# Four weight sums in buffers of their own, and a ring of three places for the rounded weights of the feed-forwards

## The reference

```python
def swiglu(h, w_in, w_out):
    g, u = jnp.split(h @ w_in, 2, axis=-1)
    return (jax.nn.silu(g) * u) @ w_out

def decoder_layer(x, c, params, ...):
    mod = jax.nn.silu(c) @ mod_w + mod_b          # 9 x 1024 columns of modulation
    ...
    h = modulate(rmsnorm(x, norm_pre[0]), sh0, sc0)
    x = x + 0.5 * gt0 * rmsnorm(swiglu(h, ffn1_in, ffn1_out), norm_post[0])
    ...                                           # token mixing, then swiglu again
```

## Time and profile before

| | us |
|---|---|
| three runs: median (range) | 3004.87 (3000.71 to 3007.12) |
| profiled execution, its own time | 2993.15 |
| its span | 2991.4 |
| the four feed-forwards within it | 427.6, 428.3, 422.9, 402.9 |

### The profile page before, as it was taken

One profiled execution on the slowest core, in us unless ns is written; L12 is line 12 of the kernel. 1 busy time (PEld: TensorE's weight loads), 2 busy tenths in 40 slices (PEclk: granted clock), 3 DMA queues, 4 the chain that ended last, 5 costly groups with the idle time before them and its releaser, 6 DMA issues.

```text
span 2991.4 us, 52877 instructions
## 1 busy us (share of the span) xinstructions
PE 2748.0 (92%) x21498; PEld 2534.2 (85%) x21498; DVE 2072.3 (69%) x3716; ACT 1205.2 (40%) x2025; POOL 802.0 (27%) x591
## 2 busy tenths in 40 slices
PE   6999989999999998999898899999999999898988
PEld 4898988898776798899888898989987768898987
DVE  2656577887877576655785656888877956857574
ACT  4433234545363253332343332445543523433232
POOL 4141322133053031414131414130420520424230
PEclk8999999999999989999999999999999999899999
DMA  7555453222224343544533444441212333332432
GB/s 255 156 169 172 142 165 101 86 59 62 64 66 134 117 129 113 171 140 136 148 99 114 155 129 125 135 134 50 64 51 66 97 115 118 99 99 59 111 79 92
DMA packets 451724, 342.19 MB, mean 114 GB/s; under 512 B 24793, under 2 KB 403025, under 8 KB 449690
## 3 DMA queue, kind: packets, MB, share of 16 engines
q1 hardware_dynamic: 446074, 313.64, 35.3%
q0 software_dynamic: 5408, 25.17, 2.5%
HBM read 319.00 MB, written 19.76 MB: 113 GB/s over the span
## 4 chain that ended last, share of the span: by engine, by line
PE 51%; DVE 26%; issue 9%; DMA 7%; ACT 5%; SPq 0%; POOL 0%; ACTq 0%; DVEq 0%; POOLq 0%
PE PS L1482 51%; DMA stage<-in_ffn_in 5%; DVE lo_apart L2176 3%; ACT w_hi L992 3%; DVE hidf L2399 2%; DVE lo_over L2176 1%; DVE score L2801 1%; DVE best L2800 1%; DVE xT L2275 1%; DVE tmpn L2273 1%; DVE sq L2284 1%; DVE h_full L2322 1%; DVE W L2731 1%; DVE hid L2336 1%; DVE sil L2404 1%
## 5 line engine op out<-in xcount | busy, mean ns | idle before, releaser
L1482 PE MATMUL PS<-h_hi,w_hi 128*128 128x260 f32 x2720 | 702.4, 301 | 49.8 <-DVE hidf L2396 15.2
L1482 PE MATMUL PS<-h_lo,w_hi 128*128 128x260 f32 x2720 | 672.3, 290 | 0.0
L2176 DVE TENSOR_TENSOR lo_apart<-stage,w_hi 128x1024 fp32r<-128x1024 f32 (+1 forms) x312 | 482.6, 1550 | 272.1 <-ACT w_hi L992 270.6
L992 ACT ACTIVATE w_hi<-stage 128x1024 fp32r<-128x1024 f32 (+2 forms) x450 | 442.0, 990 | 482.5 <-PE PS L1482 233.7
L1482 PEld LDWEIGHTS PS<-h_hi,w_hi 128*128 128x128 f32 x2720 | 485.6, 197 | 99.4 <-issue 46.7
L1482 PEld LDWEIGHTS PS<-h_lo,w_hi 128*128 128x128 f32 x2720 | 485.7, 197 | 0.0
L1482 PE MATMUL PS<-hid,w_hi 128*128 128x260 f32 x2816 | 453.3, 283 | 8.0 <-DVE hid L2336 8.0
L1482 PE MATMUL PS<-h_hi,lo_apart 128*128 128x260 f32 x1536 | 431.6, 295 | 0.0
L1482 PEld LDWEIGHTS PS<-hid,w_hi 128*128 128x128 f32 x2816 | 385.6, 188 | 11.7 <-DVE hid L2336 9.3
L3207 POOL TENSOR_TENSOR sum<-stage 128x1024 f32<-128x1024 f32 x40 | 95.8, 2394 | 795.4 <-DMA stage<-in_ffn_in 412.0
L1482 PEld LDWEIGHTS PS<-h_hi,lo_apart 128*128 128x128 f32 x1536 | 300.8, 202 | 0.0
(11 more groups left out here) (470 smaller groups left out, 5234.1 us busy)
## 6 DMA issues: line engine op xcount, KB each, us to landing
stage<-in_ffn_in SPq DMA_DIRECT2D x176, 512.0 KB, 5.2
mod_stage<-in_mod_w SPq DMA_DIRECT2D x128, 512.0 KB, 6.1
stage<-in_w_in SPq DMA_DIRECT2D x72, 512.0 KB, 3.8
stage<-in_ffn_out SPq DMA_DIRECT2D x64, 512.0 KB, 6.0
x_hold<-xT SPq DMA_DIRECT2D x6, 2080.0 KB, 6.8
stage<-in_ffn_out SPq DMA_DIRECT2D x32, 384.0 KB, 3.4
mod_open<-in_mod_w SPq DMA_DIRECT2D x16, 512.0 KB, 9.7
stage<-in_w_out SPq DMA_DIRECT2D x16, 512.0 KB, 3.6
```

The lines of the kernel that those rows point to most:

```text
L992: nc.scalar.activation(by_tile(highs(ch), ch), weights(ch), ACT.Copy).then_inc(hi_done, 1)
L1482: return nc.tensor.matmul(out, lhsT, rhs, start=start, stop=stop)
L2176: nc.vector.tensor_tensor(by_tile(lows(ch), ch), weights(ch), by_tile(highs(ch), ch).bitcast(FP32), ALU.subtract).then_inc(lo_done, 1)
```

## The change

Every feed-forward chunk gets its place in the rings from the planner. Direct trips still use places 0 to 3; win trips and output tiles use places 0, 1, 2 in turn (number modulo 3). Chunk n is then rounded when PE has used chunk n-3. ACT and DVE run two chunks ahead and not three. The fourth place of `w_hi` holds the new `sum3`, the fourth place of `lo_apart` the new `sum4`. So S3 and S4 no longer overwrite staged weights: gate slots are free after the remainder of A12, up slots after that of A22, both only when all four sums are formed. SP still loads 1, 3, 0, 2. POOL waits for all four tiles before its first sum; S4 waits no longer for the remainder of A12; after a direct trip or output tiles, S3 waits until PE has used every earlier chunk. The turns move behind A12 (`turns[1]`) and behind S4 (`turns[5]`).

```diff
+    def in_ring(ch, slot):
+
+        ch.ring_slot, ch.after = slot, rounded_last[slot]
+        rounded_last[slot] = ch.base + 1
+        ring.append(ch)
...
                     for kind in OPERANDS:
-                        ring.append(Chunk(len(ring), BLK, kind, trip=t))
+                        in_ring(Chunk(len(ring), BLK, kind, trip=t), len(ring) % 3)
                     for q in range(4):
-                        freed[q] = ('lo', t.ring + (5 if q % 2 else 6))
+                        freed[q], summed[q] = ('lo', t.ring + (5 if q % 2 else 2)), SUMS * win_count
                     if pending is not None:
-                        t.turns[0], pending = pending, None
+                        t.turns[1], pending = pending, None
                     for j in ((), (6,), (3, 6))[per_trip[trip_no]]:
                         if pending is not None:
-                            t.turns[4], pending = pending, None
+                            t.turns[5], pending = pending, None
...
             for _ in range(KD):
-                staged(n * P)
+                staged(n * P, slot=len(ring) % 3)
...
+    sum3 = over("sum3", [P, 2, 512], ring0 + 7 * BLK * 4)
+    sum4 = over("sum4", [P, 2, 512], big0 + 3 * BLK * 4)
...
+                    if load.sums is not None:
+                        sp.wait_ge(sums_formed, load.sums)
...
-                    if ch.base >= 4:
-                        act.wait_ge(chunk_used, ch.base - 3)
+                    if ch.after is not None:
+                        act.wait_ge(chunk_used, ch.after)
...
                 def win(which, t, before):
                     end = ffn_end(which)
                     for j in range(7):
-                        advance(t.ring + j + 3, end)
+                        advance(t.ring + j + 2, end)
...
-                            for slot in (1, 3):
+                            for slot in range(4):
                                 pool.wait_ge(stage_full[slot], t.loads[slot].arrival)
                             pool.tensor_tensor(sum1[:], A21, A22, ALU.add).then_inc(sums_formed, 1)
-                            for slot in (0, 2):
-                                pool.wait_ge(stage_full[slot], t.loads[slot].arrival)
+                            if t.prev != 'win':
+                                pool.wait_ge(chunk_used, t.ring)
+                            pool.tensor_tensor(sum3[:], A11, A21, ALU.subtract).then_inc(sums_formed, 1)
                             pool.wait_ge(sums_formed, n + 1)
-                            pool.tensor_tensor(A21, A11, A21, ALU.subtract).then_inc(sums_formed, 1)
                             pool.tensor_tensor(sum2[:], sum1[:], A11, ALU.subtract).then_inc(sums_formed, 1)
                             pool.wait_ge(sums_formed, n + 3)
-                            pool.wait_ge(lo_done, t.ring + 2)
-                            pool.tensor_tensor(A12, A12, sum2[:], ALU.subtract).then_inc(sums_formed, 1)
+                            pool.tensor_tensor(sum4[:], A12, sum2[:], ALU.subtract).then_inc(sums_formed, 1)
```

More of the change, by code:

```diff
@@ L132, in staged @@
         ch.load = load
-        freed[last] = ('used' if in_place else 'lo', ch.base + 1)
-        ring.append(ch)
+        freed[last], summed[last] = ('used' if in_place else 'lo', ch.base + 1), None
+        in_ring(ch, len(ring) % 4 if slot is None else slot)
         return ch
@@ L150, in ffn_plan @@
                 if t.kind == 'direct':
-                    for _ in range(4):
-                        staged(BLK)
+                    for q in range(4):
+                        staged(BLK, slot=q)
                     a, d = a + 2, d + 2
@@ L156, in ffn_plan @@
                     win_count += 1
-                    t.loads = {q: loaded(q) for q in (1, 3, 0, 2)}
+                    t.loads = {q: loaded(q) for q in range(4)}
                     t.y, t.x, t.v = banks
@@ L1106, in direct @@
                                              ACT.Silu).then_inc(ev_a, 1)
-                        advance(t.ring + 4 + m, end)
+                        if m == 0:
+                            advance(t.ring + 4, end)
                     operand_hi(which, 0)
@@ L1111, in direct @@
                     operand_hi(which, 1)
-                    advance(t.ring + 6, end)
                     hid_high(slice(1, 2), slice(0, TOK), hidf[:, 1:2, :], t.ed + 2)
@@ L1141, in ffn_out @@
                     for m in range(KD):
-                        advance(part.ring + m + 3, ffn_end(which))
+                        advance(part.ring + m + 2, ffn_end(which))
                         if m == 0:
```

24 lines of the change are left out of this document (12 added, 12 removed).

## The result

The changed kernel takes 3031.38 us (median of 8 runs, 3024.24 to 3036.12), the kernel before 3005.32 (8 runs, 2999.91 to 3018.06). The ratio is 1.0082, with an interval of 1.0064 to 1.0099: slower by 26 us, where 3003 was forecast and 3025 was the upper end of the range.

What follows compares the result with a forecast made beforehand. The prediction took a ring through SP, ACT and DVE, with DVE late and not PE, as the bound; -18 + 8 - 4 + 9 - 4 + 6.7 = -2.3 us on 3004.87 gave 3003, range 2975 to 3025.

Steps and rivals of the forecast that it cites:

- the first term: 18 trips within a part, with modulation: 27.4 us for 28.4, together -18 us.
- a ring of 26.8 to 27.3: Within a trip, from one landing of gate weights through DVE and POOL's work and the loads to the next, in us.
- The wait of S3's sum for PE's last output tile: Behind output tiles: the remainders' chain runs late, 2 us each four times behind parts of six, 0.3 behind parts of eight.
- S4 waits for nothing: In a trip's ring: named as one of two edits that gain, beside A22's evictions ahead of A11's remainder; no separate size.
- PE's idle time stands somewhere anyway; the turn is where it shows.: In the feed-forwards: PE would hardly get back the 82.8 us of idle time ahead of the turns.
- the gain that follows it in size: Behind each direct trip, the stretch to the second S2: 26.5 us for 31.7 on average, -5.1 each.
- the output borders: Eight stretches across output tiles: +9 us, bounds 0 to +40.
- the stop between the second and third feed-forward: ACT and DVE stop where a direct trip's first chunk shares place 0 with the last output tile: +6.7 us.
- The slower one: In each trip: the wait for A12 is longer and the clock falls behind it; +28 us, 3031; chance 0.14.
- own case: Whole kernel: 3003 us, own range 2990 to 3016, with PE idle 3.2 us ahead of A12 each trip; chance 0.52.
- The turn is as late as before: At the turns: S3 stands ahead of `modrow`, the 18 trips with modulation stay at 28.4 us; 3020; chance 0.12.
- The faster one: In the trips: the ring is shorter than worked out, towards PE's busy time; 38 us off, 2965; chance 0.22.

Runs made afterwards that it cites:

- f1: The change with the first sum waiting for the up tiles only and S4's sum waiting for A12's remainder again; 2980.1 us.
- d1: The change's ring of three places and turns, but sums as before, S3 and S4 overwriting staged weights; 2961.1 us.
- e6: The change with the small matmuls of a modulation group moved behind the next trip's A11; 3026.6 us.
- f3: The change with only S4's sum waiting for A12's remainder again; 3035.4 us.
- e7: The change with POOL's first sum waiting for the two up tiles only, the second for the gate tiles; 3011.6 us.
- b1: The kernel before with only the turns moved, behind A12 and behind S4; 2958.7 us.
- e4: The change with the third feed-forward's direct trip using places 3, 0, 1, 2 instead of 0, 1, 2, 3; 3031.0 us.
- e5: The change with direct trips' first three chunks in the turn of three, the fourth in place 3, and A12 rounded within the direct trip; 3018.5 us.
- e2: The change with POOL's sum S2 waiting for the remainder of A12; 3065.1 us.

## Why the prediction was wrong

The forecast for the profiled execution was 2990.9, and it took 3031.0. Of these 40 us, 22 are in the first term and 18 in the others and the rest; some 12 need not be the change's, as said above.

**The step that failed in the sum: a trip with modulation was put at 27.4 us, by a ring of 26.8 to 27.3; it took 28.6, 18 times.** The ring was too short in three places, read from the trace after:

- *The wait of S3's sum for PE's last output tile.* The prediction priced it across the output tiles only (that term came out right). It also moves the next loads. It shows best without modulation. In the 2 stretches that begin with the first trip of a part the loads used to go out 1.8 us ahead of S2's start and now go out 1.6 us after it, and the stretch took 23.8 us and takes 27.7; in the other 4 they go out 0.9 us after it (1.2 before the change), for 27.8 us and 26.7. The mean of 25.7 in the earlier trace rows hid that these are two kinds. With modulation the 6 stretches of the first kind take 29.7 us each, the other 12 take 28.0. f1 against d1 puts this wait at 14.9 us over the 8 stretches. The two differ in more than this wait, but their other 16 stretches are equal; the wait alone was not tried.
- *The half-speed A12.* The prediction had it end at 14.0 us, "which S3 (ready 13.9) and the ring don't feel". That is the 4.3 us of the earlier trace rows, where the clock rose within the product; here it stayed at 0.50 for all of it, 5.2 us. It ended 15.0 after the landing (1303.9 against POOL's start at 1288.95), and S2 starts 18.6 us after the landing. On average of the 18 trips that is 17.4 us, against 16.6 in plain trips and 16.8 in the working. e6 shows that it can't be won back by itself: 5 or 6 of the 22 us.
- *The landing.* It is 10.2 us behind the first issue on average of the 24 trips (10.3 to POOL's first sum), where 9.3 to 9.8 was taken from few trips.

**The buffers' waits.** The prediction named "S4 waits for nothing" as one of two gains in the ring. It is none anywhere: in the change it brings nothing (f3), and with an early first sum it costs 31.5 us (e7 against f1). The first sum behind the landing was counted as a loss, but it seemed to cost little, because everything else also alternated; it costs 55 us by itself (f3 against f1).

**The reasoning that failed: "PE's idle time stands somewhere anyway; the turn is where it shows."** Moving the turns alone is worth 43 us (b1). The argument held the feed-forwards with modulation against the one without and found the difference covered by the modulation's own work. But the trip without modulation leaves PE 25.7 - 22.1 = 3.6 us idle, and the 2.7 us of modulation would fit in there; a trip should have stayed near 26 us, not 28.4. The comparison had already found the loss and took it for work. With this error mended alone the forecast would have been lower still, so it does not explain why the time came out above it. But it hid that the first term is the difference of two large parts, -32 us for the turns (18 trips, 28.4 to 26.6) and +37 for the rest of the change (26.6 to 28.6). That the forecast missed by 28 us and not by more is luck: two parts that it did not see nearly cancel.

**What was right.** The chain of the ring, within 0.2 us at each of four points in a plain trip; the alternation of DVE and POOL; PE's wait behind the direct trips (the row below; "nearly 7" was forecast); the gain that follows it in size (20.8 us, 20.4 forecast), though 11.0 of it come with the turns alone (b1: 115.6 for 126.6) and not with the ring; the output borders; the stop between the second and third feed-forward (9 instead of 6.7; e4 and e5 show that it is the shared place); and what is late next, A12's remainder.

```profile
1128.38 0.56 PE L1494 MATMUL PS<-h_hi,w_hi 128*128 128x260 f32 x1 [6.91 <-DVE lo_apart L2187]
```

**The rivals.** The slower one gave 3031, which is what was measured, but not by its mechanism: no further turn at the port is lost in a trip, and PE's wait ahead of A12 (47 us in 18 trips, 2.6 each) is shorter than the 3.2 of the own case. Its condition on the clock was right, its price for it (nothing) was not. "The turn is as late as before" is refuted by the 7.0 us. The faster one named the right sign for the turns (14 half-speed products, 20 us; b1 shows 14 us from the clock); it was outvoted by the comparison with the fourth feed-forward.

## What to carry to other kernels

Suppose that one stretch has added work and a wait at it, and a like stretch without that work has idle time enough to hold the work. Then the wait is a real loss, even if the two differ by no more than the work. Where two engines take turns at a port, a wait that holds one of them back can be what keeps the critical one short, so before a wait is removed as needless, look at who asks for the port next. The same wait was worth 31.5 us in one order of the sums and nothing in another, so price such waits together. A wait priced in one stretch can cost in the next, through the loads that it holds back. When buffers change which slot comes free first, the order of the loads has to change with them: here that one line was worth 91 us.

## What the runs showed of the hardware

The end of a load can be much slower than the rest of it. The transfer rate after, between 2740 and 2752 us, in slices of 0.3 us, for one set of four tiles (2 MB):

```profile
DMA  0000024999999999999999999999951000000000
GB/s 0 0 0 0 10 68 114 261 316 374 326 323 324 317 295 295 292 287 294 287 292 294 288 289 292 288 292 292 277 145 32 19 19 19 19 7 0 0 0 0
```

Some 1.5 us run at 19 GB/s, about a sixteenth of the 290 before, in packets of 512 bytes one behind the other. That one of the 16 DMA engines is late and all wait for it fits this, but the trace doesn't name the engine of a packet. From the first issue to POOL's first sum it takes 9.4 to 9.7 us in 10 of the 24 trips within a part and 10.5 to 11.4 in 12. In 9 of those 12 the last 1.5% of the packets take over 1 us, as here; in the other 3 all of the data is late.

The half clock follows the longest wait of PE around the trip: it sat on A12 before (14 of 18 trips, behind the turn), on S3 in 6 trips of b1 (behind the turn), on A12 in 9 of the change, on S3 in 17 of 24 in e2 and on A11 in 13 of 18 in e6.

SP issues the first load of a trip 0.03 us after the remainder of A22 has ended, in all 24 trips within a part, before, after, in f1 and in d1.
